# A two-layer bidirectional encoder on one core: two of the recurrence's nine grams taken as sums by a matrix of ones

## The reference, cut to what matters

```python
def step(state, inp):
    qx, kx, lfx, vx = inp
    b = jnp.cumsum(lfx, axis=2)
    rel = b[:, :, :, None, :] - b[:, :, None, :, :]
    decay = jnp.exp(jnp.where(causal, rel, -jnp.inf))
    scores = jnp.einsum('bhtk,bhsk,bhtsk->bhts', qx, kx, decay)
    o = (jnp.einsum('bhts,bhsv->bhtv', scores, vx)
         + jnp.einsum('bhtk,bhkv->bhtv', qx * jnp.exp(b), state))
...
o_f = gla_chunk_scan(qh, k_f, lf_f, vh)
o_b = flip(gla_chunk_scan(flip(qh), flip(k_b), flip(lf_b), flip(vh)))
o = o_f + o_b
```

## Time and profile before

| | |
|---|---|
| median of 3 runs | 2179.8 us (2179.28 to 2180.06) |
| the profiled execution | 2179.53 us, span 2177.7 us |
| TensorE matmul, busy | 2163.1 us (99%) |
| TensorE weight load, busy | 1807.2 us (83%) |
| VectorE, busy | 1481.0 us (68%), 2121 instructions |
| ScalarE, busy | 1063.1 us (49%), 1041 instructions |
| GpSimd, busy | 1298.5 us (60%), 591 instructions |
| TensorE's granted clock, mean | 0.999 of 2.4 GHz |

### The profile page before, as it was taken

How to read it: one execution, slowest core, us unless ns; L and a number is a source line. 1 busy time by engine, 2 the same in 40 slices (tenths; PEclk the granted TensorE clock), 3 DMA queues, 4 the chain that set the end, 5 groups by cost and what they waited for, 6 DMA issues and landing times.

```text
span 2177.7 us, 25782 instructions
## 1 busy us (share of the span) xinstructions
PE 2163.1 (99%) x10094; PEld 1807.2 (83%) x10094; DVE 1481.0 (68%) x2121; ACT 1063.1 (49%) x1041; POOL 1298.5 (60%) x591
## 2 busy tenths in 40 slices
PE   9999999999999999999999999999999999999998
PEld 7888888888888888888878888888888888888887
DVE  6872789878666785654378637888796566865633
ACT  5434344446556554434454434345466566544443
POOL 4455544446685768666544555443576857776664
PEclk9999999999999999999999999999999999999999
DMA  8555445444445444655565554454545444546554
GB/s 318 192 194 194 172 174 177 152 174 178 171 173 175 173 174 166 252 194 186 190 213 193 193 192 174 171 178 144 185 174 175 173 174 167 181 164 252 194 189 150
DMA packets 59608, 403.66 MB, mean 185 GB/s; under 512 B 6752, under 2 KB 6880, under 8 KB 12000
## 3 DMA queue, kind: packets, MB, share of 16 engines
q1 hardware_dynamic: 59344, 401.98, 51.3%
q10 hardware_dynamic: 144, 0.03, 0.0%
HBM read 397.79 MB, written 4.19 MB: 185 GB/s over the span
## 4 chain that ended last, share of the span: by engine, by line
PE 91%; DVE 4%; ACT 2%; POOL 2%; issue 1%; DMA 0%; SPq 0%; DVEq 0%; POOLq 0%; ACTq 0%
PE acc L1219 84%; PE side L1219 6%; DVE arena L902 1%; DVE w_lo L452 1%; ACT w_hi L449 1%; POOL arena L574 0%; DVE arena L1012 0%; POOL arena L577 0%; DMA raw<-w_stream 0%; DVE wide L902 0%; POOL w_lo L452 0%; PE side L1386 0%; POOL arena L575 0%; POOL arena L594 0%; DVE arena L1022 0%
## 5 line engine op out<-in xcount | busy, mean ns | idle before, releaser
L452 POOL TENSOR_TENSOR w_lo<-raw,w_hi 128x768 fp32r<-128x768 f32 x367 | 1053.8, 2872 | 843.2 <-ACT w_hi L449 843.0
L449 ACT ACTIVATE w_hi<-raw 128x2048 fp32r<-128x2048 f32 x366 | 701.0, 1915 | 975.2 <-PE acc L1219 968.1
L452 DVE TENSOR_TENSOR w_lo<-raw,w_hi 128x1280 fp32r<-128x1280 f32 (+1 forms) x371 | 586.4, 1581 | 596.4 <-ACT w_hi L449 593.9
L1219 PE MATMUL acc<-w_hi,xT_hi 128*128 128x512 f32 x2112 | 654.3, 392 | 1.9 <-DVE w_hi L937 1.1
L1219 PE MATMUL acc<-w_hi,xT_lo 128*128 128x512 f32 x2112 | 647.8, 389 | 0.0
L1219 PE MATMUL acc<-w_lo,xT_hi 128*128 128x512 f32 x2112 | 528.3, 392 | 3.3 <-DVE w_lo L452 3.0
L1219 PEld LDWEIGHTS acc<-w_hi,xT_lo 128*128 128x128 f32 x2112 | 396.4, 188 | 83.5 <-DVE xT_lo L428 0.2
L1219 PEld LDWEIGHTS acc<-w_lo,xT_hi 128*128 128x128 f32 x2112 | 391.9, 188 | 83.8 <-DVE w_lo L452 4.6
L1219 PEld LDWEIGHTS acc<-w_hi,xT_hi 128*128 128x128 f32 x2112 | 392.5, 188 | 81.6 <-DVE w_hi L937 1.4
L902 DVE STREAM_TRANSPOSE arena<-stage 32x256 f32<-32x256 f32 (+1 forms) x480 | 204.7, 427 | 7.1
L1219 PEld LDWEIGHTS side<-arena 128*128 128x128 f32 x864 | 118.3, 191 | 11.9 <-DVE arena L1049 2.3
(11 more groups left out here) (149 smaller groups left out, 1926.4 us busy)
## 6 DMA issues: line engine op xcount, KB each, us to landing
raw<-w_stream SPq DMA_DIRECT2D x367, 1024.0 KB, 4.8
x_out<-arena SPq DMA_DIRECT2D x16, 256.0 KB, 2.7
arena<-x_turned_in SPq DMA_DIRECT2D x4, 512.0 KB, 8.4
arena<-x_in SPq DMA_DIRECT2D x2, 1024.0 KB, 15.9
arena<-x_in SPq DMA_DIRECT2D x4, 512.0 KB, 5.6
wide<-post_in SPq DMA_DIRECT2D x2, 1024.0 KB, 7.1
arena<-x_out SPq DMA_DIRECT2D x4, 512.0 KB, 5.6
raw<-w_stream SPq DMA_DIRECT2D x2, 512.0 KB, 5.9
```

The costliest lines, as they stand in the source:

```text
L449: return act.activation(w_hi[:, g % 2, :], raw[:, g % LANDING, :], ACT.Copy)
L452: return eng.tensor_tensor(w_lo[:, g % LANDING, cols], raw[:, g % LANDING, cols], w_hi[:, g % 2, cols].bitcast(F32), ALU.subtract)
L1219: return pe.matmul(out, a, b, start=start, stop=stop)
```

## The change

1. Level -1 and level 0 are no longer grams. Both need a single key for each query (the token itself, or its neighbour), so VectorE multiplies queries and keys element by element (two instructions: one at d = 4, one at d = 7 on 256 elements), ScalarE rounds the 512 products per partition to fp32r (`products_high`, at d = 5 and d = 8), VectorE takes the remainder (`products_low`, same passes), and TensorE sums over the partitions by a stationary 128x128 matrix of ones: two fp32r matmuls of 512 columns. Every row of the result is the same; for level -1 VectorE multiplies it by the identity where it copied before, for level 0 the mask picks.
2. Level 0's sum is taken one step later, together with level 1's gram; VectorE keeps both at d = 9, and nothing at d = 8.
3. ScalarE's and TensorE's waits are rewritten to fit (`mixed` counts eight per unit now; `paired`, `pair_hi`, `pair_lo` are new).
4. `TURN_A` goes from `UNITS[7] + 7` to `+ 9`, 58 to 60: branch A's two passes of transposes to 60 and 61, its split to 62.
5. `ones`, written once at the start; `products_hi` and `products_lo` lie in `wide`.

```diff
-TURN_A = UNITS[A_UNITS - 1] + 7
+TURN_A = UNITS[A_UNITS - 1] + 9
...
+                def products_high(u, l):
+                    act.wait_ge(S.paired, 2 * u + l + 2)
+                    if u or l == 0:
+                        act.wait_ge(S.grams, (LEVELS + 1) * u + 1 if l == 0 else (LEVELS + 1) * (u - 1) + 2)
+                    act.activation(products_hi, EQ[:, 1] if l < 0 else EQ[:, 3], ACT.Copy).then_inc(S.pair_hi, 1)
...
                             if d == 5:
+                                products_high(u, -1)
                                 act.wait_ge(S.rec_prep, 2 * u + 2)
...
-                                    act.wait_ge(S.grams, (LEVELS + 1) * u + l)
+                                    if l == 1:
+                                        products_high(u, 0)
+                                    elif l == 2:
+                                        act.wait_ge(S.paired, 2 * u + 2)
+                                    else:
+                                        act.wait_ge(S.grams, (LEVELS + 1) * u + l)
                                     act.wait_ge(S.scanned, (LEVELS - 1) * u + l)
...
+                def products_low(u, l):
+                    products = EQ[:, 1] if l < 0 else EQ[:, 3]
+                    dve.wait_ge(S.pair_hi, 2 * u + l + 2)
+                    dve.tensor_tensor(products_lo, products, products_hi.bitcast(F32), ALU.subtract).then_inc(S.pair_lo, 1)
...
-                                dve.tensor_tensor(keys(-1), EQ[:, 0], EQ[:, 1], ALU.add).then_inc(S.mixed, 1)
+                                link(dve.tensor_tensor(keys(-1), EQ[:, 0], EQ[:, 1], ALU.add))
+                                dve.tensor_tensor(keys(-1), keys(-1), q, ALU.mult).then_inc(S.paired, 1)
+                            if d == 5:
+                                products_low(u, -1)
...
+                                for n in {0: [0], 1: [], 2: [1, 2]}.get(l, [l]):
+                                    dve.wait_ge(S.grams, nine + n + 1)
...
+                                if l == 1:
+                                    products_low(u, 0)
+                                    dve.wait_ge(S.pair_lo, 2 * u + 2)
 
                                 dve.wait_ge(S.decays, LEVELS * u + l + 1)
                                 dve.tensor_tensor(EQ[:, 3], q, EQ[:, 0], ALU.mult).then_inc(S.mixed, 1)
+                                if l == 0:
+                                    dve.wait_ge(S.mixed, LEVELS * u + 1)
+                                    dve.tensor_tensor(crossed(EQ[:, 3], 0, 1, 0), crossed(EQ[:, 3], 0, 1, 0),
+                                                      crossed(keys(0), 1, -1, 0), ALU.mult).then_inc(S.paired, 1)
...
+                        for level in {0: [], 1: [0, 1]}.get(l, [l] if -1 <= l < LEVELS else []):
+                            yield u, level
...
+                        if l <= 0:
+                            pe.wait_ge(S.pair_hi, 2 * u + l + 2)
+                            mm(dst, ones[:, :], products_hi, stop=False)
+                            pe.wait_ge(S.pair_lo, 2 * u + l + 2)
+                            mm(dst, ones[:, :], products_lo, start=False).then_inc(S.grams, 1)
+                            continue
+                        pe.wait_ge(S.mixed, LEVELS * u + l + 1)
```

More of the change, by code:

```diff
@@ L168, in build @@
         stage = sb("stage", [P, MT, CW])
-        wide = sb("wide", [P, 1028 + 1024])
+        wide_place = nc.sbuf_base
+        wide = sb("wide", [P, 1028 + 1028])
         scores = wide[:, 0:1028]
@@ L176, in build @@
         probsT_a = [probsT[:, b * A_COLS:(b + 1) * A_COLS] for b in range(2)]
+        products_hi = nc.alloc_sbuf_tensor_at("products_hi", [P, 512], F32R, offset=wide_place + 4 * 512)[:, :]
+        products_lo = nc.alloc_sbuf_tensor_at("products_lo", [P, 512], F32R, offset=wide_place + 4 * 1544)[:, :]
         ropes = sb("ropes", [P, 2, MT * 4 * ROT])
@@ L186, in build @@
         warm = sb("warm", [P, P])
+        ones = sb("ones", [P, P], F32R)
         def piece(at, shape, dt=F32):
@@ L291, in build @@
             staged roped turned tanhed scored masked probs probs_turned probs_copied attended
-            normed branch_turned branch_hi branch_lo lb_ready rec_prep rec_exp logs_ready mixed grams
+            normed branch_turned branch_hi branch_lo lb_ready rec_prep rec_exp logs_ready mixed paired pair_hi pair_lo grams
             decays scanned kept rec_out rec_squared rec_rstd_ready rec_y gated summed out_half out_squared out_summed
@@ L929, in _ @@
                 dve.memset(warm[:, :], 0.0).then_inc(warm_ready, 1)
+                dve.wait_ge(warm_ready, 1)
+                dve.tensor_scalar(ones[:, :], warm[:, :], 0.0, 1.0, ALU.mult, ALU.add)
                 for layer in range(DEPTH):
@@ L1034, in _ @@
                             if 0 <= l < LEVELS:
[L1036 to L1044, removed]
-                                    ins = dve.copy_predicated(S_diag, lmasks[:, l - 1:l, :].broadcast_to([P, 4, P]), src)
@@ L1046, in _ @@
-                                ins.then_inc(S.kept, 1)
+                                for n in {0: [0], 1: [], 2: [1, 2]}.get(l, [l]):
+                                    dve.wait_ge(S.grams, nine + n + 1)
+                                    src = side[0][:, (nine + n) % 2 * 512:(nine + n) % 2 * 512 + 512].rearrange(
+                                        "p (b t) -> p b t", t=P)
+                                    if n == 0:
+                                        if u:
+                                            dve.wait_ge(S.rec_out, u)
+                                        ins = dve.tensor_tensor(S_diag, ident[:, None, :].broadcast_to([P, 4, P]), src, ALU.mult)
+                                    else:
+                                        dve.wait_ge(S.kept, nine + n)
+                                        ins = dve.copy_predicated(S_diag, lmasks[:, n - 1:n, :].broadcast_to([P, 4, P]), src)
+                                    ins.then_inc(S.kept, 1)
@@ L1318, in last_two_steps, with grams_of, level_grams @@
                         renewed(layer + 1, 1)
-                def level_grams(s):
+                def grams_of(s):
                     for u in range(4):
                         l = s - 1 - REC[u] - FIRST_LEVEL
-                        if not -1 <= l < LEVELS:
-                            continue
-                        q = rec_views(u)[0]
+                        for level in {0: [], 1: [0, 1]}.get(l, [l] if -1 <= l < LEVELS else []):
+                            yield u, level
+                def level_grams(s):
+                    for u, l in grams_of(s):
                         n = (LEVELS + 1) * u + l + 1
-                        pe.wait_ge(S.mixed, n + 1)
                         if n >= 2:
```

6 lines of the change are left out of this document (3 added, 3 removed).

## The result

| | before | after |
|---|---|---|
| median | 2179.5 us (4 runs, 2179.3 to 2180.1) | 2206.7 us (4 runs, 2206.0 to 2206.9) |
| ratio | | 1.0124, 95% interval 1.0112 to 1.0136 |
| span of the profiled execution | 2177.7 us | 2204.2 us |
| VectorE, busy | 1481.0 us | 1551.6 us |
| TensorE's granted clock, mean | 0.999 | 0.995 |

What follows compares the result with a forecast made beforehand. TensorE, holding 91% of the chain, bounds the kernel. Per layer -3.6 (grams) - 0.45 (turn) + 2.2 (unit 0) + 0.5 (unit 1) + 3.3 (unit 3) = +1.95, both layers +3.9: 2183.4 us, range 2175.5 to 2188.5.

Steps and rivals of the forecast that it cites:

- grams: TensorE, both levels: sixteen grams become pairs of fp32r matmuls, saving 0.9 us per unit, 3.6 per layer.
- turn A: Branch A's turn moved: the 1.3 us wait at step 61 goes, 0.85 returns at step 64; gain 0.45 per layer.
- `w_hi` before 102 and 132: TensorE waits for late `w_hi`: 0.5 us in unit 1, 1.5 (1.65 with restart) in unit 3.
- unit 0, levels: Unit 0: L1049's product comes late for the gram of step 90; 2.2 us lost with earlier wait and restarts.
- unit 1, levels: Unit 1: no VectorE transposes of chunks, nothing late from the levels; no loss, covered by the 5.7 us lead.
- unit 3, levels: Unit 3: level-1 product late at step 134, 2.05 us with restart, less 0.4 that step 135 lost before.
- unit 2, levels: Unit 2: no VectorE transposes of chunks, nothing late from the levels; no loss, covered by the 5.7 us lead.
- Part 1: TensorE's work: two fp32r matmuls of 512 columns replace each gram, 0.45 us instead of 0.90.
- Part 2: Branch A's turn, steps 58 to 64: gain 0.45 us per layer, 1.3 if rope instructions didn't wait for GpSimd.
- Part 3: ScalarE's queue at d = 5: copy waits for `paired`; `w_hi` loses 1.5 us unit 3, 0.5 unit 1, under 0.1 unit 0.
- Part 4: Levels: VectorE 1.4 us later before d = 7, plus neighbours' product 0.45; late products at steps 90 and 134.
- Rival 3: Slower: added two-SBUF-input instructions land on GpSimd's, 1.70 instead of 0.69, at steps 90 and 134: 2187 to 2190; chance 0.18.

Runs made afterwards that it cites:

- the queue's wait alone: Kernel before with the turn at 60, plus one ScalarE copy per unit ahead of the logarithms at d = 5, waiting for VectorE's L1023: 2189.4 us.

## Why the prediction was wrong

The sum was right where it followed a queue and wrong where it took durations for fixed. By its parts, layer 0, from the lengths of the steps:

| | predicted | measured |
|---|---|---|
| grams | -3.6 | -3.24 |
| turn A | -0.45 | -1.29 |
| `w_hi` before 102 and 132 | 0.5 + 1.65 | 0.46 + 1.52 |
| unit 0, levels | 2.2 | 7.1 |
| unit 1, levels | 0 | 1.5 |
| unit 3, levels | 1.65 | 6.8 |
| unit 2, levels | 0 | 0.2 |
| sum | +1.95 | +13.1 |

The 0.3 us between this sum and layer 0's 13.4 are small differences at other steps.

- **Part 1** was right in kind. Two matmuls with ones cost 0.50 in the length of a step, not 0.45.
- **Part 2** took the lower end. I had counted the rope instructions at 4.1, their length before, with a `w_lo` of GpSimd beside two of them; with the turn moved they take 2.6. The bound of 1.3, for rope instructions that GpSimd doesn't hold up, held.
- **Part 3**, the wait in ScalarE's queue, was right to 0.15 us at both places. The table load has no drain behind it here either: L814 starts 0.01 us after it. So the 2.8 us more that followed from the Trainium skill, "ScalarE: Activation LUTs", section What ACT_TABLE_LOAD costs, did not come. But the step that failed starts here. The part ended at TensorE's wait for `w_hi`, and called unit 0 covered at under 0.1. It did not ask what else the late `w_hi` feeds. It feeds GpSimd, whose two `w_lo` then stand together beside L1029. The kernel with the queue's wait alone shows that the late queue costs 12.5 us, of which the forecast's path, TensorE's wait for `w_hi`, is some 1.6. Another 6.4 go when GpSimd is held. The other 4.5 stay at steps 133 and 134, where one of the two meetings is left.
- **Part 4** moved VectorE's work by its own added time, 1.4 us, and kept each duration from before. In the trace of after `w_lo`, L1029, L1049 and `products_lo` changed theirs: VectorE is busy 70.6 us more, where the added instructions, at what they were priced, make some 20. The neighbours' product was also sized wrongly: it has 512 elements in two halves of 256, and takes 1.22 to 1.41 instead of 0.45, each time with GpSimd beside it. "Units 1 and 2: I find nothing late" was wrong for unit 1, where both L1029 take 2.33 and step 104 loses 1.4.
- **The clock** was taken as fixed: no part of the sum has a term for it. At steps 89 and 134 it fell, and cost 1.45 and 1.67 us, and it fell at the same steps of layer 1.
- **Rival 3** named the right mechanism and had 0.18. It was priced from L1049 at 1.0 a hit and with one or two hits a layer. L1029 was the line to look at: its own view shows that in the kernel before 4 of its 16 took 2.33, in units 1 and 2, where there was room for it. A hit costs 1.6, and after the change 14 of the 16 are hit. With two hits at unit 3 and one more each at units 0 and 1, as in the trace of after, the rival would have come to 2183.4 + 2 x 6.4 = 2196 us. That is an estimate, as if every hit reached TensorE in full. Some 6 of the 10 that are still missing are the clock's; the rest is in instructions that were not priced one by one.

The accounts don't close piece by piece. Queue alone costs 12.5, VectorE's part of level -1 with the copies at d = 6 10.9, both together 15.9. My reading is that either one produces much the same meetings, and having both doesn't double them; no run shows it. Step 89 isn't taken apart either: it is at 6.35 and 6.85, its ideal, with level -1 or level 0 alone, and at 12.22 with both. Not tried: the added work put on GpSimd, and a cheaper form of the neighbours' product.

## What to carry to other kernels

A wait put into one engine's queue has to be followed past the engine that waits for it next: here ScalarE was late, so that GpSimd ran two instructions in one go, and these lay over VectorE's critical one. Before trusting a duration, look at its least, median and longest over all places: a line that takes 0.74 at the tight places and 2.33 at the loose ones tells what happens when the timing shifts. And a saving per unit is to be taken only in the units that have room for its side work: with the copies at d = 6 it gave 0.8 us per unit and layer in two of four, and cost 6.4 and 6.0 us in the other two (layer 0).

## What the runs showed of the hardware

- TensorE's granted clock can fall to 0.50 behind waits as short as 0.84 + 0.84 us within 2.2 us, and can stay at 1.00 behind the same or behind a single 2.5. Between the same step of the two layers, one with a fall and one without, the difference was 1.3 (11.45 and 10.11, step 89 with the copies at d = 6), 1.6 (10.62 and 9.05) and 2.4 us (13.18 and 10.74, step 134 with GpSimd held).
- VectorE's L1029 (SCALAR_TENSOR_TENSOR, 128x512, two SBUF inputs) takes 0.74 us with no GpSimd instruction beside it and 2.33 with GpSimd's 128x768 subtraction beside it.
- `products_lo` (TENSOR_TENSOR, 128x512, also two SBUF inputs) took 0.68 to 0.69 us in all ten places of after where no GpSimd instruction lay beside it, and 1.32 to 2.35 in the six others.
- Lying beside each other is not a hit by itself. In the kernel before, 32 of the 64 L1049, which have two SBUF inputs too, took 0.67 to 0.70 us with over 0.5 us of a GpSimd instruction beside them. No run here shows what decides it.
- In the kernel before, in 25 of 33 places the activation behind a table load starts 0.01 us after it; in the eight others it waits for VectorE.
